# The MLP's first product as seven block products per pair of strips, in a split-fp32 transformer trunk on one Trainium2 core

## What is computed

```python
h = x + pool_mixer(rms_norm(x)) ;  h = h + sqrelu_mlp(rms_norm(h))     # layer 0
k, v = shared_kv(rms_norm(h))
h = h + diff_attention(rms_norm(h), k, v) ;  h = h + sqrelu_mlp(rms_norm(h))   # layer 1
return rms_norm(h)

def sqrelu_mlp(h, w_in, w_out):          # w_in 2048 x 8192, w_out 8192 x 2048
    u = jax.nn.relu(h @ w_in)
    return (u * u) @ w_out
```

## Time and profile before

| | us |
|---|---|
| median of 3 runs | 1876.15 (1875.76 to 1877.27) |
| profiled execution, its own time | 1876.52 |
| its span, first to last instruction | 1873.9 |
| TensorE busy | 1848.4 (99%) |
| VectorE busy | 1147.2 (61%) |
| ScalarE busy | 837.4 (45%) |
| matmuls of 512 columns | 7776 |

### The profile page before, as it was taken

One profiled execution on the slowest core, in us unless ns is written; L12 is line 12 of the kernel. 1 busy time (PEld: TensorE's weight loads), 2 busy tenths in 40 slices (PEclk: granted clock), 3 DMA queues, 4 the chain that ended last, 5 costly groups with the idle time before them and its releaser, 6 DMA issues.

```text
span 1873.9 us, 24428 instructions
## 1 busy us (share of the span) xinstructions
PE 1848.4 (99%) x8425; PEld 1536.3 (82%) x8425; DVE 1147.2 (61%) x1406; ACT 837.4 (45%) x1057; POOL 10.9 (1%) x15
## 2 busy tenths in 40 slices
PE   6999999999999999999999999999999999999998
PEld 5888888888888888888888888888888888888886
DVE  7656665655656556755557777565655555555666
ACT  6544444444444444644345545444444444444443
POOL 0000000000000000000000000000000000000000
PEclk9999999999999999999999999999999999999999
DMA  7555565655555565555554446556555555555553
GB/s 276 191 191 179 182 198 186 194 182 198 181 191 188 190 195 180 167 195 198 187 195 149 138 151 214 179 181 192 188 191 192 195 191 189 185 190 190 179 181 110
DMA packets 178441, 348.17 MB, mean 186 GB/s; under 512 B 10642, under 2 KB 10852, under 8 KB 178020
## 3 DMA queue, kind: packets, MB, share of 16 engines
q1 hardware_dynamic: 177696, 345.88, 56.7%
q10 hardware_dynamic: 708, 1.81, 0.3%
HBM read 345.55 MB, written 2.10 MB: 186 GB/s over the span
## 4 chain that ended last, share of the span: by engine, by line
PE 95%; DVE 3%; issue 1%; ACT 1%; DMA 1%; POOL 0%; SPq 0%; DVEq 0%; POOLq 0%; ACTq 0%
PE bank L942 30%; PE bank L940 30%; PE bank L941 30%; PE bank L958 2%; DVE w_lo L603 1%; DMA h<-in_x 0%; PE bank L1100 0%; DVE h L649 0%; DVE a_lo L627 0%; PE bank L993 0%; PE bank L992 0%; PE bank L994 0%; DVE b_lo L716 0%; DMA raw<-in_pool_w 0%; DVE w_lo L708 0%
## 5 line engine op out<-in xcount | busy, mean ns | idle before, releaser
L377 ACT ACTIVATE w_hi<-raw 128x1024 fp32r<-128x1024 f32 x640 | 669.5, 1061 | 806.2 <-PE bank L942 801.2
L603 DVE TENSOR_TENSOR w_lo<-raw,w_hi 128x1024 fp32r<-128x1024 f32 x640 | 764.9, 1221 | 307.9 <-ACT w_hi L377 304.1
L940 PE MATMUL bank<-w_hi,a_hi 128*128 128x512 f32 x1344 | 527.6, 393 | 0.0
L942 PE MATMUL bank<-w_hi,a_lo 128*128 128x512 f32 x1344 | 523.3, 389 | 0.0
L941 PE MATMUL bank<-w_lo,a_hi 128*128 128x512 f32 x1344 | 523.1, 389 | 0.0
L940 PE MATMUL bank<-w_hi,b_hi 128*128 128x512 f32 x1216 | 475.7, 391 | 0.0
L942 PE MATMUL bank<-w_hi,b_lo 128*128 128x512 f32 x1216 | 473.3, 389 | 0.0
L941 PE MATMUL bank<-w_lo,b_hi 128*128 128x512 f32 x1216 | 473.1, 389 | 0.0
L649 DVE TENSOR_TENSOR h<-bank,h 128x512 f32<-128x512 f32 x280 | 180.4, 686 | 220.2 <-PE bank L942 220.2
L942 PEld LDWEIGHTS bank<-w_hi,a_lo 128*128 128x128 f32 x1344 | 252.3, 188 | 52.6
L941 PEld LDWEIGHTS bank<-w_lo,a_hi 128*128 128x128 f32 x1344 | 252.5, 188 | 50.9
(11 more groups left out here) (94 smaller groups left out, 424.9 us busy)
## 6 DMA issues: line engine op xcount, KB each, us to landing
raw<-in_w_mlp_in SPq DMA_DIRECT2D x256, 512.0 KB, 3.7
raw<-in_w_mlp_out SPq DMA_DIRECT2D x256, 512.0 KB, 4.8
raw<-in_w_kv SPq DMA_DIRECT2D x64, 512.0 KB, 4.1
raw<-in_w_q SPq DMA_DIRECT2D x32, 512.0 KB, 5.0
raw<-in_w_o SPq DMA_DIRECT2D x32, 512.0 KB, 4.1
raw<-in_pool_w SPq DMA_DIRECT2D x8, 512.0 KB, 7.6
h<-in_x SPq DMA_DIRECT2D x4, 512.0 KB, 6.3
scratch<-in_pool_scale ACTq DMA_DIRECT2D x1, 1024.0 KB, 6.6
```

The costliest lines, as they stand in the source:

```text
L377: nc.scalar.activation(w_hi[:, n], raw[:, n % RAW], ACT.Copy).then_inc(hi_ready, 1)
L603: nc.vector.tensor_tensor(w_lo[:, n], raw[:, n % RAW], w_hi[:, n].bitcast(F32), ALU.subtract).then_inc(lo_ready, 1)
L940: nc.tensor.matmul(banks[tb][:], hi[:, tok], w_hi[:, n, kk, :], start=begin, stop=False)
L942: last = nc.tensor.matmul(banks[tb][:], lo[:, tok], w_hi[:, n, kk, :], start=False, stop=end)
```

## The change

**Input product.** Columns of w_in are taken in pairs of strips (1024), and rows in quarters of K: per pair of strips three "mixed units" and one "plain unit" of K 512 each. In a mixed unit the 256 x 512 activations are 2 x 2 blocks (tokens by K halves of 256), the 512 x 1024 weights 2 x 2 blocks a, b (upper rows, left and right columns) and c, d (lower rows). VectorE makes four sums in the raw buffers: a + b, b + d, then d + (a + b), then c + that. Seven block products (P1 to P7; banks B_P1 ...), each 128 tokens x K 256 x 512 columns, that is 2 k tiles x 3 = 6 matmuls, take the place of eight. The plain unit does the last quarter of K as before (48 matmuls), straight into four of the banks. The seven activation blocks (three plain, four sums, S1 to S4) are made once a layer, at its entry, into `mix_hi`, `mix_lo`. After the pair, eight additions (`c_11`, `c_rest`) combine the banks into four hidden blocks, which ScalarE takes through relu and square (two instructions each) with no VectorE part.

**Lots.** A "lot" is now 2048 elements wide (two slots) in one instruction on ScalarE and on VectorE, but for lot 0 of a mixed unit (block a alone, 1024). A mixed unit has lots 0 (a), 1 (c and d), 2 (the sums a', b'), 3 (the sums c', d'): 8 slots of the ring; 6, 12, 12 and 12 matmuls. The plain unit has 2 lots, the output of a pair 8, of 24 matmuls each. Raw buffers are eight in two halves of four; a half is loaded for a whole unit, two buffers at a time.

**Output product.** For a pair K 1024 is summed in PSUM before the addition into h, so there are four groups a pair, with 8 additions of 512 columns, not 16.

**Order.** Pair p: units 1, 2, plain, 3 of its input, then the output of pair p - 1, then its own turning (16 transposes). Pair 0 has the plain unit first. VectorE does the last two h additions of the output before (`out_add` 2 and 3) and the split of u (`u_low`) in unit 1. The last pair's output stands as two strips, as before.

The core of the diff:

```diff
+            def load_unit(half, sources, free_ab, free_cd, order=(0, 1, 2, 3)):
+                for i in order:
+                    if free_ab is not None and i in (order[0], order[2]):
+                        sp.wait_ge(lo_ready, free_ab if i < 2 else free_cd)
+                    sp.dma_start(raw_half[half][:, i], sources[i]).then_inc(raw_landed[RAW * half + i], 16)
...
+            def hi_pair(at, slot, half, cd, landed):
+                for i in (2 * cd, 2 * cd + 1):
+                    act.wait_ge(raw_landed[RAW * half + i], landed * 16)
+                act.wait_ge(pe_done, at - 6)
+                nc.scalar.activation(w_hi[:, slot:slot + 2], raw_half[half][:, 2 * cd:2 * cd + 2], ACT.Copy).then_inc(hi_ready, 2)
...
+            def mix_hi_lots(at, slot, half, landed, sums, lots):
+                for lot in lots:
+                    spot = (slot + 2 * lot) % HALVES
+                    if lot == 0:
+                        act.wait_ge(raw_landed[RAW * half], landed * 16)
+                        act.wait_ge(pe_done, at - 7)
+                        nc.scalar.activation(w_hi[:, spot], raw_half[half][:, 0], ACT.Copy).then_inc(hi_ready, 2)
+                    elif lot == 1:
+                        hi_pair(at + 2, spot, half, 1, landed)
+                    elif lot == 2:
+                        hi_sums(at + 4, spot, half, 0, sums + 2)
+                    else:
+                        hi_sums(at + 6, spot, half, 1, sums + 4)
...
-            def u_hi(j, layer, at):
-                for b in range(2):
-                    act.wait_ge(t_ready, 2 * (j + R_U[layer]) + b + 1)
-                    nc.scalar.activation(b_hi[:, at + 2 * b:at + 2 * b + 2, :], T[b][:].rearrange("p (c t) -> p c t", c=2),
-                                         ACT.Copy).then_inc(t_hi, 1)
+            def round_u(layer, p, last):
+                for b in range(4):
+                    act.wait_ge(u_turned, (p + 8 * layer) * 4 + (b + 1))
+                    nc.scalar.activation(u_tiles(2 * b, last)[0], U_BANKS[b][:].rearrange("p (c t) -> p c t", c=2), ACT.Copy).then_inc(u_rounded, 1)
...
-            def u_square(j, layer, banks):
-                for tb in range(TB):
-                    dve.wait_ge(relu_done, (j + NJ * layer) * TB + tb + 1)
-                    nc.vector.scalar_tensor_tensor(hidden[:, tb], banks[tb][:], rms[:, 2 * layer + 1, tb:tb + 1], relu[:, tb],
-                                                   ALU.mult, ALU.mult).then_inc(hidden_done, 1)
+            def mix_lo_lots(at, slot, half, landed, sums, lots):
+                a, b, c, d = (raw_half[half][:, i] for i in range(4))
+                for lot in lots:
+                    spot = (slot + 2 * lot) % HALVES
+                    if lot == 0:
+                        dve.wait_ge(hi_ready, at + 2)
+                        nc.vector.tensor_tensor(w_lo[:, spot], a, w_hi[:, spot].bitcast(F32), ALU.subtract).then_inc(lo_ready, 2)
+                        dve.wait_ge(raw_landed[RAW * half + 1], landed * 16)
+                        dve.wait_ge(lo_ready, at + 2)
+                        nc.vector.tensor_tensor(a, a, b, ALU.add).then_inc(w_summed, 1)
+                    else:
+                        lo_pair(at + 2 * lot, spot, half, lot % 2)
+                    if lot == 1:
+                        nc.vector.tensor_tensor(b, b, d, ALU.add).then_inc(w_summed, 1)
+                        dve.wait_ge(w_summed, sums + 2)
+                        dve.wait_ge(lo_ready, at + 4)
+                        nc.vector.tensor_tensor(d, d, a, ALU.add).then_inc(w_summed, 1)
+                        dve.wait_ge(w_summed, sums + 3)
+                        nc.vector.tensor_tensor(c, c, d, ALU.add).then_inc(w_summed, 1)
...
+            def c_rest(layer, p):
+                done = (p + 8 * layer) * 8
+                dve.wait_ge(pe_done, i_at(layer, p) + 28)
+                nc.vector.tensor_tensor(hid_12, B_P6[:], p1_copy, ALU.add).then_inc(c_added, 1)
+                dve.wait_ge(c_added, done + 2)
+                nc.vector.tensor_tensor(hid_21, B_P7[:], hid_12, ALU.add).then_inc(c_added, 1)
+                dve.wait_ge(c_added, done + 3)
+                nc.vector.tensor_tensor(hid_22, B_P5[:], hid_21, ALU.subtract).then_inc(c_added, 1)
+                nc.vector.tensor_tensor(hid_12, B_P5[:], hid_12, ALU.subtract).then_inc(c_added, 1)
+                dve.wait_ge(c_added, done + 4)
+                nc.vector.tensor_tensor(hid_21, B_P4[:], hid_21, ALU.add).then_inc(c_added, 1)
+                dve.wait_ge(c_added, done + 5)
+                nc.vector.tensor_tensor(hid_12, B_P3[:], hid_12, ALU.add).then_inc(c_added, 1)
+                nc.vector.tensor_tensor(hid_22, B_22[:], hid_22, ALU.add).then_inc(c_added, 1)
...
+                mix_lo_lots(at, slot, 0, i_landed(layer, p, 0), sums, (0,))
+                if second:
+                    c_11(layer, 0)
+                else:
+                    out_add(layer, p - 2, 2)
+                mix_lo_lots(at, slot, 0, i_landed(layer, p, 0), sums, (1,))
+                if second:
+                    c_rest(layer, 0)
+                mix_lo_lots(at, slot, 0, i_landed(layer, p, 0), sums, (2,))
+                if not second:
+                    out_add(layer, p - 2, 3)
+                u_low(layer, p - 1, False)
+                mix_lo_lots(at, slot, 0, i_landed(layer, p, 0), sums, (3,))
+                mix_lo_lots(at + 8, slot, 1, i_landed(layer, p, 1), sums + 4, range(4))
+                for cd in range(2):
+                    lo_pair(at + 16 + 2 * cd, slot + 2 * cd, 0, cd)
+                mix_lo_lots(at + 20, (slot + 4) % HALVES, 1, i_landed(layer, p, 3), sums + 8, range(4))
...
+            def product(bank, hi, lo, slot, kk, begin, end):
+                nc.tensor.matmul(bank[:], hi, w_hi[:, slot, kk, :], start=begin, stop=False)
+                nc.tensor.matmul(bank[:], hi, w_lo[:, slot, kk, :], start=False, stop=False)
+                return nc.tensor.matmul(bank[:], lo, w_hi[:, slot, kk, :], start=False, stop=end)
+            def mixed(bank, which, u, slot, begin, end):
+                r = 2 * (u - 1)
+                for kk in range(2):
+                    last = product(bank, mix_hi[:, which, r + kk, :], mix_lo[:, which, r + kk, :], slot, kk,
+                                   begin and kk == 0, end and kk == 1)
+                return last
...
+                pe.wait_ge(lo_ready, at + 2)
+                if fresh and steady:
+                    pe.wait_ge(h_added, p * 4 + (hb - 5))
+                elif fresh:
+                    pe.wait_ge(p1_copied, 8 * layer + 1)
+                mixed(B_P1, MIX_11, u, slot, begin, end).then_inc(pe_done, 2)
+                pe.wait_ge(lo_ready, at + 4)
+                if fresh and not steady:
+                    pe.wait_ge(c_added, 64 * layer + 1)
+                mixed(B_P2, MIX_12, u, (slot + 2) % HALVES, fresh, end).then_inc(pe_done, 1)
+                if fresh and steady:
+                    pe.wait_ge(h_added, p * 4 + (hb - 4))
+                elif fresh:
+                    pe.wait_ge(c_added, 64 * layer + 7)
+                mixed(B_P3, MIX_S4, u, (slot + 3) % HALVES, fresh, end).then_inc(pe_done, 1)
+                pe.wait_ge(lo_ready, at + 6)
+                mixed(B_P5, MIX_S1, u, (slot + 4) % HALVES, begin, end).then_inc(pe_done, 1)
+                if fresh and not steady:
+                    turn_u(layer, 0)
+                if first and begin:
+                    pe.wait_ge(t_taken, 2 * (R_H[2 * layer] + 3) + 2)
+                elif begin:
+                    pe.wait_ge(u_taken, done - 3)
+                mixed(B_P7, MIX_S3, u, (slot + 5) % HALVES, begin, end).then_inc(pe_done, 1)
+                pe.wait_ge(lo_ready, at + 8)
+                if fresh:
+                    pe.wait_ge(u_taken, done - 2)
+                mixed(B_P4, MIX_22, u, (slot + 6) % HALVES, fresh, end).then_inc(pe_done, 1)
+                if fresh:
+                    pe.wait_ge(u_taken, done - 1)
+                mixed(B_P6, MIX_S2, u, (slot + 7) % HALVES, begin, end).then_inc(pe_done, 1)
...
+            def in_pair(layer, p, par):
+                at, slot = i_at(layer, p), 4 * par
+                mix_unit(layer, p, 1, at, slot, True, False)
+                mix_unit(layer, p, 2, at + 8, slot, False, False)
+                std_unit(layer, p, at + 16, slot)
+                mix_unit(layer, p, 3, at + 20, (slot + 4) % HALVES, False, True)
...
-                with nc.tensor.Fori(1, NJ - 1) as j:
-                    out_strip(s0 + 2 * j, U_FIRST, layer, j - 1, lambda g: None)
-                    pe.wait_ge(hidden_done, (j + NJ * layer + 1) * TB)
-                    for g in range(NG):
-                        in_group(s0 + 2 * j + 1, g, a_tile, X)
-                        if g == 1:
-                            turn_u(j, layer)
+                with nc.tensor.Fori(1, 3) as it:
+                    for c in range(2):
+                        in_pair(layer, it * 2 + c, c)
```

(2 more changed lines are left out.)

700 lines of the change are left out of this document (500 added, 200 removed).

## The result

The changed kernel takes **1920.94 us** (1917.87 to 1922.16, four executions) against 1876.71 us for the kernel before: 1.023 times as long, interval 1.021 to 1.025. The forecast was 1901 in a range of 1881 to 1924: the direction and the range hold, but the loss is 44 us, not 25.

What follows compares the result with a forecast made beforehand. TensorE, busy for 99% of the span, was taken as the bound. 1876.5 - 65.3 (removed matmuls) + 34.2 (steady waits) + 29.3 + 27.3 (layer entries) - 0.3 (earlier entry wait) = 1901.7; forecast median 1901 us, range 1881 to 1924.

Steps and rivals of the forecast that it cites:

- The saved matmuls: Input product: 18 fewer matmuls per pair, 288 in all at 0.2268 us each, 65.3 us off TensorE.
- the steady period: Length of one of pairs 2 to 7: 84.76 us of TensorE work plus a 2.85 us wait, 87.6 us.
- VectorE's price: VectorE's time for a mixed unit: 12.7 us against TensorE's 9.5, with 2.30 us for a 2048-element subtraction alone.
- the steady wait: Pairs 2 to 7: TensorE waits 2.85 us once a pair at lot 2 of the second mixed unit, 34 us in all.
- the pair's zero: Steady pairs: the moment when TensorE issues past the last output matmul, from which the forecast counts its times.
- The weight loads: Loads of w_in: same size and number as before, 4.1 us median to landing, issued a unit ahead, no loss.
- Elsewhere: Outside steady pairs and entries: weight loads, end groups, K/V, Q and attention add nothing; a loop turn costs under 1 us.
- The rival that named this place: Unit 3's c and d arrive late for ScalarE, 4 us a pair over 12 pairs: 1950 us; chance 0.04.
- The entries: Pairs 0 and 1 of each layer: TensorE waits for VectorE 29.3 us in the first layer, 27.3 in the second.
- the smaller lag: Second layer's entry: the O strip leaves VectorE about 2 us less behind, so 27.3 us of waits, not 29.3.
- the clock falls in the waits: Rival: TensorE drops to 1.2 GHz after waits, about 1.5 us each, up to 30 us in all: 1931 us; chance 0.06.
- the prediction's own last sentence: Signs of error: 2048-element row below 2.1 us, TensorE waits in unit 3 or more for block additions, clock below full level.

Runs made afterwards that it cites:

- The kernel with the filled wait: Changed kernel plus 11 unneeded TensorE products of 512 columns at lot 2 of the second mixed unit, pairs 2 to 7: 1905.27 us.
- two thirds of the saving with no steady wait: Changed kernel with two mixed and two plain units a pair: 1862.92 us; the same with pair 0's block additions before the last sum in pair 1: 1860.31 us.

## Why the prediction was right, and where it was off

**The saved matmuls** were sized rightly: the full pace is 0.2268 us a matmul in both kernels, and the steady period with an unhurt wait is 87.5 us, where I had 87.6.

**VectorE's price** was right: 2.288 us for the 2048-element subtraction against 2.30 taken, 2.20 against 2.22 in a row, and 1.26 for a dependent sum. (The Trainium skill's figure that the prediction quotes, 2291 ns from "VectorE: DVE Perf Modes", section on the TRN2 errata, agrees with the row.) ScalarE's copy is 1.91, not 2.01.

**Place and size of the steady wait** were right: lot 2 of the second mixed unit ready 17.9 us after the pair's zero against 17.95; the wait with its restart is 222.14 - 219.32 - 0.23 = 2.6 us against 2.85. Lot 3, the plain unit, the last mixed unit and the output halves have no wait, as worked out.

**The weight loads** were not what the forecast said of them. Under "Elsewhere" it had them land in time; in the rows c and d of the last mixed unit keep ScalarE idle for 3.0 to 4.9 us in every steady pair. The rival that named this place had the mechanism, but took the longest landing and so a cost of 4 us a pair (its own figures give 4.9). In this kernel the slack takes all of the lateness, and the cost to TensorE is nothing.

**The entries** came out at 30.0 and 30.5 us against 29.3 and 27.3. Pair 2 begins at 204.2, where the prediction had 203.7. The sum of their waits is smaller (22.9 and 18.5): VectorE sets these stretches, as argued, and slow matmuls fill a part of the time in which TensorE would otherwise have waited. They aren't free, though. The kernel with the filled wait has the same code up to pair 2, and there 37 starts of matmuls are 0.40 to 0.44 us apart instead of 10, the waits are 3.3 us shorter, and pair 2 begins 2.5 us later (206.7). The second entry, 3.2 us longer than forecast, has 34 such starts and 4.4 us less of waits than the first, so the smaller lag that the forecast gave it was there and the clock took it back; that last step is argued, no run separates the two.

**The step that failed** is the clock behind the waits, which the forecast's sum put at nothing. It stood as the rival "the clock falls in the waits": its mechanism was right, its price too (1.5 us written, 1.4 in the rows), its chance was not: 0.06. The argument against it was that a wait of 0.88 us in the earlier trace rows left the pace whole and that mine were under 3.2. The trace of before has one longer wait that I didn't use, with the full pace behind it too:

```profile
1086.91 0.84 PE L1116 MATMUL bank<-keep,probs 128*128 128x128 f32 x6 [1.72 <-DVE scratch L887]
```

Between 1.72 and 4.93 us it has no wait of TensorE at all, and I let the short ones speak for all of that gap. Of the ten intervals between steady pairs, eight show the loss. In the prediction's own terms: mean periods of 88.68 and 88.65 us instead of 87.6 give 12 x 1.07 = 12.8 us, the entries 3.9 more than forecast, and 1901.7 + 12.8 + 3.9 = 1918.4, against 1917.87 for this execution. That the time still lies in the range is in part luck. The 22 us above the forecast were meant for other terms (a dearer subtraction, a steady wait or an entry wrong by some us), and the clock took 17 of them; the prediction's own last sentence counts a granted clock that leaves its full level as a sign that it is wrong. The other three executions are 2.6 to 4.3 us longer at mean granted clocks of 0.977 to 0.980 against 0.983 here.

**Left open.** Why the clock stays whole behind one wait of 2.8 us from start to start (pair 6 of either layer) and falls behind another of the same length isn't settled; only that standing still is the cause is shown. The second half of the change, the output product over K 1024 with half as many additions into h, was not tried alone; VectorE is ahead in the output halves, and with the sums left out the steady pairs take TensorE's work and no more, so the rows give no sign that it matters by itself.

## What to carry to other kernels

When matmuls are traded for work on another engine, lay the other engine's queue out against TensorE's wishes stretch by stretch: 73 us of work in 84.8 fitted on average, and the steady pairs still lost 50 us, since a lead can't be larger than the ring of buffers holds. Price each wait of TensorE of 2 to 3 us as the wait plus a slow stretch behind it (1.3 to 1.4 us here, behind ten of twelve). And take the trade only as far as the helper keeps pace: two thirds of the saving with no steady wait gave 13 to 16 us, all of it lost 44.

## What the runs showed that I had not expected

Waits of TensorE of about 2.4 us were followed by some seven matmuls at the 1.2 GHz level in ten of twelve pairs, while waits of 1.4 us in the kernel with the plain unit second were not. Moving 234 us of additions from VectorE to GpSimd cost 127 us, since each takes twice as long there and the two engines take turns. And useless work for TensorE in place of a wait can pay: 132 unneeded matmuls made the kernel 16 us faster, by the clock alone.
